# Sums over 0/1 matrices from a high and a low part, and the opening's squares added on VectorE

## What is computed

```python
def rms_norm(x, g):                      # the first one opens the kernel
    y = xf * lax.rsqrt(jnp.mean(xf * xf, axis=-1, keepdims=True) + EPS)

def forgetting_attention(qkv, ...):      # 8 heads of 64
    q = rms_norm(q.reshape(b, s, ATTN_HEADS, HEAD_DIM), q_g)
    k = rms_norm(k.reshape(b, s, ATTN_HEADS, HEAD_DIM), k_g)

def stick_breaking_attention(q, k, v):   # 4 heads of 128
    ln = jnp.where(before, jax.nn.log_sigmoid(-z), 0.0)
    within = jnp.einsum('bhqcj,ji->bhqci', lnc, tri_within)
    after = ...                          # sums of whole 128-key chunks that come later
    logw = z + lnc + within + after
```

## Time and profile before

| | |
|---|---|
| median of 3 runs | 2933.48 us (2933.28 to 2933.89) |
| profiled execution | 2933.4 us, its span 2931.4 us |
| TensorE busy | 2918.3 us |
| VectorE busy | 1924.0 us |
| ScalarE busy | 1511.1 us |
| GpSimd busy | 239.6 us |
| memory traffic | mean 186 GB/s over the span |

### The profile page before, as it was taken

How to read it: one execution, slowest core, us unless ns; L and a number is a source line. 1 busy time by engine, 2 the same in 40 slices (tenths; PEclk the granted TensorE clock), 3 DMA queues, 4 the chain that set the end, 5 groups by cost and what they waited for, 6 DMA issues and landing times. The chain is left out here.

```text
span 2931.4 us, 48844 instructions
## 1 busy us (share of the span) xinstructions
PE 2918.3 (100%) x17288; PEld 2570.4 (88%) x17288; DVE 1924.0 (66%) x2206; ACT 1511.1 (52%) x1896; POOL 239.6 (8%) x199
## 2 busy tenths in 40 slices
PE   9999999999999999999999999999999999999999
PEld 7888898998888888888888888988888888888888
DVE  7696765567665656656655666655787567757775
ACT  5576644454544444444544446555665455545564
POOL 3010020102101010000200000001000000010021
PEclk9999999999999999999999999999999999999999
DMA  8566667665655666556565555556565666666555
GB/s 244 165 184 185 173 182 224 184 180 188 199 187 186 193 189 191 188 184 194 179 198 182 166 160 169 186 184 208 160 202 179 200 187 186 191 188 187 185 159 172
DMA packets 543862, 545.94 MB, mean 186 GB/s; under 512 B 17304, under 2 KB 542112, under 8 KB 543744
## 3 DMA queue, kind: packets, MB, share of 16 engines
q1 hardware_dynamic: 540576, 536.79, 59.7%
q0 software_dynamic: 2480, 7.10, 0.9%
q10 hardware_dynamic: 688, 0.53, 0.1%
HBM read 542.25 MB, written 2.11 MB: 186 GB/s over the span
## 5 line engine op out<-in xcount | busy, mean ns | idle before, releaser
L1648 DVE TENSOR_TENSOR w_low<-raw,w_high 128x1024 fp32r<-128x1024 f32 x1012 | 1261.6, 1260 | 777.6 <-ACT w_high L1082 772.5
L1082 ACT CAST w_high<-raw 128x1024 fp32r<-128x1024 f32 x1012 | 1050.0, 1048 | 996.7 <-PE ps_gemm L704 961.5
L699 PE MATMUL ps_gemm<-act_a,w_high 128*128 128x512 f32 x4448 | 1434.0, 395 | 6.1 <-DVE act_a L1879 2.0
L699 PE MATMUL ps_gemm<-act_b,w_high 128*128 128x512 f32 x3208 | 1044.3, 395 | 0.0
L704 PEld LDWEIGHTS ps_gemm<-act_a,w_low 128*128 128x128 f32 x4608 | 861.7, 188 | 152.0
L704 PE MATMUL ps_gemm<-act_a,w_low 128*128 128x256 f32 x4608 | 991.7, 279 | 0.0
L704 PE MATMUL ps_gemm<-act_b,w_low 128*128 128x256 f32 x3520 | 778.8, 279 | 0.0
L699 PEld LDWEIGHTS ps_gemm<-act_a,w_high 128*128 128x128 f32 x4448 | 713.2, 188 | 53.2 <-issue 7.2
L704 PEld LDWEIGHTS ps_gemm<-act_b,w_low 128*128 128x128 f32 x3520 | 652.5, 189 | 96.9
L699 PEld LDWEIGHTS ps_gemm<-act_b,w_high 128*128 128x128 f32 x3208 | 524.4, 188 | 42.4
L1718 DVE TENSOR_TENSOR summ<-ps_gemm,bcopy 128x512 f32<-128x512 f32 x220 | 150.4, 684 | 8.8 <-ACT bcopy L1097 8.8
(11 more groups left out here) (287 smaller groups left out, 1217.8 us busy)
## 6 DMA issues: line engine op xcount, KB each, us to landing
raw<-in_w_in SPq DMA_DIRECT2D x348, 512.0 KB, 4.2
raw<-in_w_up SPq DMA_DIRECT2D x176, 512.0 KB, 3.5
raw<-in_w_mlp_up SPq DMA_DIRECT2D x128, 512.0 KB, 3.9
raw<-in_w_mlp_down SPq DMA_DIRECT2D x128, 512.0 KB, 3.5
raw<-in_w_down SPq DMA_DIRECT2D x88, 512.0 KB, 3.5
raw<-in_w_out SPq DMA_DIRECT2D x64, 512.0 KB, 4.6
raw<-in_w_branch SPq DMA_DIRECT2D x32, 512.0 KB, 3.7
raw<-in_w_ple_gate SPq DMA_DIRECT2D x32, 512.0 KB, 3.5
```

Of the source, the lines that this page charges most:

```text
L699: nc.tensor.matmul(ps[:, g, t, :], wh[:, at, o:o + P], x, start=first, stop=False, skip_group_check=True)
L1082: nc.scalar.copy(wh[:, at, :], raw[:, at, :]).then_inc(high_ready, 1)
L1648: nc.vector.tensor_tensor(wl[:, at, :], raw[:, at, :], wh[:, at, :].bitcast(F32), ALU.subtract).then_inc(split_done, 1)
```

## The change

Opening: ScalarE squares tiles 0 to 3 and 4 to 7 at their old places, none in the third step, and 8 to 11 and 12 to 15 after the fourth. VectorE adds tiles 4 to 7 to 0 to 3 at the end of the third step, and behind the first piece of `proj_a` the other two adds. TensorE sums the four remaining tiles with four f32 products. GpSimd adds nothing and waits for VectorE's third add before it goes on.

First attention, rounds 0 to 2: ScalarE rounds the 512 squares to fp32r (`sq_high`), VectorE subtracts (`sq_low`) between its two weight pieces, and TensorE multiplies both by an fp32r copy of `same_head`. Round 3 is as before.

Stick-breaking: the masked logarithms are split likewise (`l_high`, `l_low`), and TensorE makes six fp32r products out of three f32 ones. The 0/1 matrices are copied to fp32r once. The parts lie in places that are free at the time (`wf_s`, tiles 14 and 15 of `act_b`, 12 and 13 of `act_a`).

```diff
@@ TensorE
-            ssq(0, sq0_added, 8)
+            pe.wait_ge(sq0_added, 3)
+            for c in range(4):
+                last = nc.tensor.matmul(pm[:, 3, 0:S], ones, G[:, 16 + c, :], start=(c == 0), stop=(c == 3))
+            last.then_inc(ssq_ready, 1)
...
                 take(fill, 2)
-                pe.wait_ge(at_sq, c + 1)
+                if c == 0:
+                    pe.wait_ge(zero_one, 1)
+                if c < 3:
+                    pe.wait_ge(at_low, c + 1)
+                else:
+                    pe.wait_ge(at_sq, c + 1)
...
-                nc.tensor.matmul(pm[:, 0, :], same_head, G[:, 16:18, :].rearrange("p o n -> p (o n)"),
-                                 start=True, stop=True).then_inc(at_ssq, 1)
+                if c < 3:
+                    nc.tensor.matmul(pm[:, 0, :], zo_head, sq_high, start=True, stop=False)
+                    nc.tensor.matmul(pm[:, 0, :], zo_head, sq_low, start=False, stop=True).then_inc(at_ssq, 1)
...
-                pe.wait_ge(s_ln, h + 1)
-                nc.tensor.matmul(pm[:, 1, 0:S], later, PJ[:, 22, :], ...)
-                nc.tensor.matmul(pm[:, 1, P:S], ones, PJ[:, 23, 0:P], ...)
-                nc.tensor.matmul(pm[:, 1, S:S + P], later, PJ[:, 23, 0:P], ...)
+                pe.wait_ge(s_low, h + 1)
+                nc.tensor.matmul(pm[:, 1, 0:S], zo_later, l_high[:, 0:S], ...)
+                nc.tensor.matmul(pm[:, 1, 0:S], zo_later, l_low[:, 0:S], ...)
+                nc.tensor.matmul(pm[:, 1, P:S], zo_ones, l_high[:, S:3 * P], ...)
+                nc.tensor.matmul(pm[:, 1, P:S], zo_ones, l_low[:, S:3 * P], ...)
+                nc.tensor.matmul(pm[:, 1, S:S + P], zo_later, l_high[:, S:3 * P], ...)
+                nc.tensor.matmul(pm[:, 1, S:S + P], zo_later, l_low[:, S:3 * P], ...)
@@ ScalarE
-                nc.scalar.activation(tiles(G, 16 + 4 * s, 4), tiles(G, 4 * s, 4), ACT.Square).then_inc(sq0_ready, 1)
+                for q in ((0,), (1,), (), (2, 3))[s]:
+                    nc.scalar.activation(tiles(G, 16 + 4 * q, 4), tiles(G, 4 * q, 4), ACT.Square).then_inc(sq0_ready, 1)
...
+                if c == 0:
+                    act.wait_ge(f_logits, 1)
+                    nc.scalar.copy(zo_head, same_head).then_inc(zero_one, 1)
                 nc.scalar.activation(G[:, 16, :], PJ[:, 20 + c, :], ACT.Square)
+                if c < 3:
+                    link(nc.scalar.activation(G[:, 17, :], PJ[:, 24 + c, :], ACT.Square))
+                    nc.scalar.copy(sq_high, G[:, 16:18, :].rearrange("p o n -> p (o n)")).then_inc(at_sq, 1)
...
+                if h == 0:
+                    act.wait_ge(in_c2, 16)
+                    nc.scalar.copy(zo_ones, ones)
+                    nc.scalar.copy(zo_later, later).then_inc(zero_one, 1)
+                act.wait_ge(s_ln, h + 1)
+                nc.scalar.copy(l_high, l3).then_inc(s_high, 1)
                 take(fill, 3)
@@ VectorE
+                if s == 2:
+                    dve.wait_ge(sq0_ready, 2)
+                    nc.vector.tensor_tensor(tiles(G, 16, 4), tiles(G, 16, 4), tiles(G, 20, 4),
+                                            ALU.add).then_inc(sq0_added, 1)
+            def squares_0():
+                dve.wait_ge(sq0_ready, 4)
+                nc.vector.tensor_tensor(tiles(G, 24, 4), tiles(G, 24, 4), tiles(G, 28, 4), ALU.add).then_inc(sq0_added, 1)
+                dve.wait_ge(sq0_added, 2)
+                nc.vector.tensor_tensor(tiles(G, 16, 4), tiles(G, 16, 4), tiles(G, 24, 4), ALU.add).then_inc(sq0_added, 1)
...
             piece(pa, 0, 0, 0)
+            squares_0()
             piece(pa, 0, 0, 1)
...
                 dve.wait_ge(y_done, 12 + c)
-                take(fill, 2)
+                take(fill, 1)
+                if c < 3:
+                    dve.wait_ge(at_sq, c + 1)
+                    nc.vector.tensor_tensor(sq_low, G[:, 16:18, :].rearrange("p o n -> p (o n)"),
+                                            sq_high.bitcast(F32), ALU.subtract).then_inc(at_low, 1)
+                take(fill, 1)
...
+                dve.wait_ge(s_high, h + 1)
+                nc.vector.tensor_tensor(l_low, l3, l_high.bitcast(F32), ALU.subtract).then_inc(s_low, 1)
                 take(fill, 2)
@@ GpSimd
-            for b in range(8):
-                ...
-                nc.gpsimd.tensor_tensor(sqacc[:], sqacc[:], tiles(G, 16 + 2 * b, 2), ALU.add).then_inc(sq0_added, 1)
-
+            pool.wait_ge(warmed, 1)
+            pool.wait_ge(sq0_added, 3)
             nc.gpsimd.memset(cbuf[:, 0:1024], 0.0).then_inc(bd_zeroed, 1)
```

More of the change, by code:

```diff
@@ L283, in build @@
         onesrow = G[:, 12, :]
+        zo_head, zo_ones, zo_later = wf_s[:, 0:P], wf_s[:, 0:P], wf_s[:, P:2 * P]
+        sq_high, sq_low = act_b[:, 15, :], act_b[:, 14, :]
+        l_high, l_low = act_a[:, 12, 0:3 * P], act_a[:, 13, 0:3 * P]
         wf_parts = wf_s[:].rearrange("p (q a n) -> p a q n", q=4, a=2)
@@ L338, in build @@
         sc_z, sc_base, sc_y = sem("sc_z"), sem("sc_base"), sem("sc_y")
+        at_low, s_high, s_low, zero_one = sem("at_low"), sem("s_high"), sem("s_low"), sem("zero_one")
         at_sq, at_ssq, at_rms, at_qk, at_vps, at_v = (
@@ L853, in _ @@
                 take(fill, 2)
-                pe.wait_ge(at_sq, c + 1)
+                if c == 0:
[4 more added lines that the diff above has]
+                    pe.wait_ge(at_sq, c + 1)
                 if c:
                     pe.wait_ge(y_high, 12 + c)
-                nc.tensor.matmul(pm[:, 0, :], same_head, G[:, 16:18, :].rearrange("p o n -> p (o n)"),
-                                 start=True, stop=True).then_inc(at_ssq, 1)
+                if c < 3:
+                    nc.tensor.matmul(pm[:, 0, :], zo_head, sq_high, start=True, stop=False)
+                    nc.tensor.matmul(pm[:, 0, :], zo_head, sq_low, start=False, stop=True).then_inc(at_ssq, 1)
+                else:
+                    nc.tensor.matmul(pm[:, 0, :], same_head, G[:, 16:18, :].rearrange("p o n -> p (o n)"),
+                                     start=True, stop=True).then_inc(at_ssq, 1)
                 if c:
@@ L1002, in _ @@
                 take(fill, 3)
-                pe.wait_ge(s_ln, h + 1)
-                nc.tensor.matmul(pm[:, 1, 0:S], later, PJ[:, 22, :], start=True, stop=False,
+                if h == 0:
+                    pe.wait_ge(zero_one, 2)
+                pe.wait_ge(s_low, h + 1)
+                nc.tensor.matmul(pm[:, 1, 0:S], zo_later, l_high[:, 0:S], start=True, stop=False,
                                  skip_group_check=True)
-                nc.tensor.matmul(pm[:, 1, P:S], ones, PJ[:, 23, 0:P], start=False, stop=True,
+                nc.tensor.matmul(pm[:, 1, 0:S], zo_later, l_low[:, 0:S], start=False, stop=False,
                                  skip_group_check=True)
-                nc.tensor.matmul(pm[:, 1, S:S + P], later, PJ[:, 23, 0:P], start=True, stop=True,
+                nc.tensor.matmul(pm[:, 1, P:S], zo_ones, l_high[:, S:3 * P], start=False, stop=False,
+                                 skip_group_check=True)
+                nc.tensor.matmul(pm[:, 1, P:S], zo_ones, l_low[:, S:3 * P], start=False, stop=True,
+                                 skip_group_check=True)
+                nc.tensor.matmul(pm[:, 1, S:S + P], zo_later, l_high[:, S:3 * P], start=True, stop=False,
+                                 skip_group_check=True)
+                nc.tensor.matmul(pm[:, 1, S:S + P], zo_later, l_low[:, S:3 * P], start=False, stop=True,
                                  skip_group_check=True).then_inc(s_suf, 1)
@@ L1320, in _ @@
                 act.wait_ge(epi_done, BY["proj_b"].unit0 + 2 + 3 + c // 2)
+                if c == 0:
+                    act.wait_ge(f_logits, 1)
+                    nc.scalar.copy(zo_head, same_head).then_inc(zero_one, 1)
                 nc.scalar.activation(G[:, 16, :], PJ[:, 20 + c, :], ACT.Square)
-                nc.scalar.activation(G[:, 17, :], PJ[:, 24 + c, :], ACT.Square).then_inc(at_sq, 1)
+                if c < 3:
+                    link(nc.scalar.activation(G[:, 17, :], PJ[:, 24 + c, :], ACT.Square))
+                    nc.scalar.copy(sq_high, G[:, 16:18, :].rearrange("p o n -> p (o n)")).then_inc(at_sq, 1)
+                else:
+                    nc.scalar.activation(G[:, 17, :], PJ[:, 24 + c, :], ACT.Square).then_inc(at_sq, 1)
                 take(fill, 2)
```

## The result

The changed kernel takes 2942.93 us (median of 7 runs, 2939.36 to 2946.39); the kernel before, on the same chip, took 2934.11 (7 runs, 2933.28 to 2935.52). The ratio is 1.003, interval 1.002 to 1.004: slower by 0.3%. The time lies inside the range of 2936.2 to 2943.0, at its upper end, 3.8 us above the forecast of 2939.1; that it is slower by over 0.2% was the likeliest of the three outcomes. It is inside the range by 0.07 us, and three of the seven runs lie above it.

The account below looks back on a forecast made before the run. TensorE, busy for 2918.3 of 2931.4 us, was taken to bound the kernel. Attention waits +8.31, opening -1.85 and stick-breaking -0.80 sum to +5.66 us on 2933.4: forecast 2939.1 us, range 2936.2 to 2943.0.

Parts of the forecast that it names:

- The waits: First attention, rounds 0 to 2: TensorE waits for VectorE's late subtraction, +2.87, +2.72 and +2.72 us, +8.31 in all.
- a new wait on TensorE is paid in full: TensorE, whole kernel: busy 2918.3 of 2931.4 us, so a new wait costs its whole length; attention clock 1.00.
- The opening: Up to the sum of squares: without GpSimd's adds VectorE's operations shorten and TensorE stops less, gain 1.85 us.
- Stick-breaking: Four heads: six split products replace three f32 ones, 0.67 for 0.87 us, -0.20 a head, -0.80 in all.
- the second rival: Stick-breaking: a split product of 128 columns costs as much as the f32 one, +0.96 us, total 2940.8; chance 0.30.
- The fourth: Stick-breaking: a split product's price goes by its columns, saving 0.41 us a head, total 2938.2; chance 0.10.
- The first rival: First attention: VectorE reaches the subtraction before TensorE arrives, -1.17 us there, total 2929.6; chance 0.10.
- The third: Opening: VectorE's operations stay long without GpSimd's adds, +2.6 us instead of -1.85, total 2943.5; chance 0.08.
- The chances: Whole kernel: slower by over 0.2% 0.52, within 0.2% 0.44, faster by over 0.2% 0.04; the forecast itself 0.38.
- the upper bound: Whole kernel: top of the range, 2943.0 us, set towards VectorE's opening operations staying long.

## Why the prediction was right, and where it fell short

- **The waits: right, in place, cause and size.** The order of VectorE's queue (a split, then the subtraction) gave +2.87, +2.72 and +2.72 net; measured +2.87, +2.65 and +2.70. Two terms were off and cancelled in round 0: VectorE's split started at 206.87, 1.26 us earlier than the 208.13 that I took from before, by exactly what TensorE gained in the opening; so the earlier gain moved both sides, as the prediction said of rounds 1 and 2 but didn't use for round 0.
- **The step that failed: "a new wait on TensorE is paid in full", with the granted clock of 1.00 taken for the whole stretch.** That clock belongs to a TensorE that never stops there. The change puts in three stops of 3 us, and the sum has no term for what the clock does behind them. The missing term measured 3.0 us in the profiled execution (two falls); by their mean clocks it was nothing in the fastest run and more in the slowest. With it the forecast of 2939.1 becomes 2942.1; of the 0.8 us that are left 0.6 are the opening, by the late piece below.
- **The opening: right in mechanism and in size; the two traces alone hide it, -1.26 for -1.85.** The operations are short, as replayed. VectorE's split of the fifth piece of `proj_0` ended at 18.87, where I had 18.31, so TensorE came to that piece at 19.42 for 18.88, to the squares at 31.34 for 30.79, and went on at 33.07 for 32.58: one lateness of half a microsecond, handed down. It is that of the piece's arrival (16.57 for 16.01), which differs from execution to execution by 0.7 us in nine traces of this opening; counted from the split's start the gain is 1.8. What the prediction left out is that a gain taken from one execution of each kernel carries this scatter.
- **Stick-breaking: right in the sum.** Three of the four 128-column split products take 0.11 to 0.12 us, as the recorded half of an f32 one does, and one takes 0.05: 0.39 us for the four where I had 0.44, and -0.19 a head for -0.20. That each costs as much as the f32 product (0.22), the second rival, is refuted by the spacing of 1779.38, 1779.49 and 1779.61. The fourth (0.058 each by columns, -0.41 a head) is refuted as a rule by the same spacing, but one product of the four does come at its price; why that one, no run shows.
- **The first rival (waits covered)** didn't hold for the order as changed, yet became true with one piece more ahead of the product. **The third (VectorE stays long)** is refuted twice: by the 486 ns in the trace after and by the 1259 ns once GpSimd adds again.
- **The chances.** 0.52 for slower held; but up to 0.38 of it lay on the second and third rivals, whose mechanisms were false. The sum of the forecast alone, +0.19%, stood within 0.2%. Slower by 0.3% came from the clock, for which no rival stood. That the outcome and the range both held is therefore in good part luck: the upper bound was meant for the third rival, and it covered the clock's 3 us by 0.07.

## What to carry to other kernels

Price a new stop on a full TensorE as its length and what the clock may lose behind it; here a stop of 3 us cost about 1.5 us more when the clock fell, 16 of the 17 runs with three such stops have a mean clock below 1.000, and with stops of 4 us it was lowest, 0.996 to 0.997 in every run. Look first whether the consumer can go one piece later or the producer one place up in its queue: each of the two takes a line or two, and together they turned +9 us into -4. Where a stop can't be avoided, products that nobody needs keep the clock, and cost nothing that these runs could tell; judge such versions by the spread of the runs as well as by the median.

## What the runs showed of the hardware that I had not expected

- The granted clock fell to 0.50 for 3.41 us at a time, and in two places for 6.83 (round 2 with the subtraction behind both pieces, round 0 with GpSimd's adds); the two stretches of 3.41 us in the change lost 1.5 us each. It came with waits of 1.4 us (once, in an opening with several), 1.8 us (near the end), 2.8 and 3.0 us in some executions and not in others, and with 4.0 and 4.2 us in all three rounds of the one execution profiled. It began anywhere from 1.6 us before the wait's end (315.5, the wait over at 317.1) to 1.9 us behind it, so the row on which the slow stretch shows can lie a piece away from the wait.
- One GpSimd stream with one tile as both inputs and output, 128x512 f32, stretches a VectorE operation of two SBUF inputs from 0.48 to as much as 1.26 us; in the kernel before, where the second input is another tile, to 1.54. No run tells whether the second tile makes that difference.

What stays open: why the same wait loses the clock in one execution and not in the next, and at which of its waits the version with the subtraction ahead lost it in nine of eleven runs.
